# Loading the norm rows ahead of the weights, and taking half of the residual work earlier, in the two output-projection stages of a fused two-model block

## The chip, the cores and the metric

The kernel runs on one core of one Trainium2 chip. The metric is the time of one execution on the device, in microseconds (us); smaller is better. All data and arithmetic are float32; matmul operands are stored as pairs of rounded fp32 parts ("hi" and "lo"), so that one product takes three matmuls.

## The reference, cut to what matters

A sequence of 256 tokens of width 1024 goes through a first block (a conformer convolution and a gated FFN) and then through two layers of a second block. Each layer is FFN, mixer, output projection, FFN. The changed code is the output projection with its residual:

```python
x = layer_norm(ALPHA * x + 0.5 * swiglu(x, ...), ln_g[i, 0], ln_b[i, 0])      # FFN 1
...                                                                          # mixer -> heads
heads = jnp.concatenate([mix, memory_attention(mq, mem_k, mem_v)], axis=-1)
x = layer_norm(ALPHA * x + heads @ w_out[i], ln_g[i, 1], ln_b[i, 1])          # output projection
x = layer_norm(ALPHA * x + 0.5 * swiglu(x, ...), ln_g[i, 2], ln_b[i, 2])      # FFN 2
```

## The kernel before, in words

The program is a row of blocks; at the end of each, all engines meet. The output projection of layer 0 (after the RWKV mixer) and that of layer 1 (after the stick-breaking mixer) are the two calls of `output_stage`, called stage A and stage B here. Both do the same work.

**Weights.** All wide weights pass through a ring of two raw buffers `a_raw[:, 0..1]` (1 MB each, 128 partitions x 2048 words). A chunk g is loaded by SyncE (`Ring.load`, L112), its hi part is made by ScalarE (a copy with rounding), its lo part by VectorE (raw minus hi), and TensorE multiplies with both. `Ring.load(g)` waits until the lo part of chunk g-2 is made, since that frees the raw buffer. The output weights `w_out` are four chunks, g0 to g0+3, called chunks 0 to 3 here. Chunks 0 and 1 were loaded and split in the stage before. In the output stage, SyncE loads chunks 2 and 3 and then chunks 4 and 5, which are the first two weight chunks of the FFN that follows (each as two DMAs of 512 KB, gate and up). The loads of chunks 2 and 3 wait for nothing in this stage; that of chunk 4 waits for the lo part of chunk 2, that of chunk 5 for the lo part of chunk 3.

**Split buffers.** The parts of chunk 2 go to `b_parts`, which is free. Those of chunk 3 take the place of chunk 1's, those of chunk 4 the place of chunk 0's. So ScalarE's hi part of chunk 3 waits until TensorE is done with chunk 1 (`ring_a.used`). ScalarE runs chunks 2, 3 and 4 in this order at L1533, VectorE follows at L1548.

**The residual.** x lies in `x_tok` (tokens on partitions, two tiles t = 0, 1) as the plain normalized value of the norm before. Its gain and bias must still be applied before `ALPHA * x` is added. For this, two rows of 1024 words, `ln_g` and `ln_b`, are loaded with a broadcast to all 128 partitions (`load_row`, L297, 512 KB written by each), and `residual(t)` does a multiply (L1539) and an add (L1540) of 128x1024 on VectorE, for each t. The buffer `rows` holds masks of the mixer in stage A until that mixer is over.

**The end of the stage.** TensorE accumulates four output blocks (t, half n). Blocks 0 to 2 are finished first, then block 3's part from chunk 2, then the transposes of token tile 0 (`turn_tokens`, L371), and only then block 3's part from chunk 3. VectorE goes on, right behind the lo part of chunk 4, with `norm_dve_side`: for each block the sum with `ALPHA * x` (L326) and its statistics (L328), then mean and variance, a square root on ScalarE (L339), a reciprocal, and the scaling of the low half (L351), for which the transposes wait. All engines run their instructions in the order of the program text.

Of the kernel before, what the change touches and what calls it, by code (L numbers as in the profile page):

```python
# [210 lines left out]
def build_program(nc, A, out):  # L211
    with ExitStack() as ctx:
# [3 lines left out]
        def sem(name):  # L216
            return ctx.enter_context(nc.semaphore(name))
# [28 lines left out]
        def carve(*shapes, limit=arena_words):  # L246

            at, got = 0, []
            for shape in shapes:
                n = math.prod(shape)  # L250
                ap = arena[:, at:at + n]
                if len(shape) == 2:
                    ap = ap.rearrange("p (a b) -> p a b", a=shape[0])
                elif len(shape) == 3:
                    ap = ap.rearrange("p (a b c) -> p a b c", a=shape[0], b=shape[1])
                got.append(ap)
                at += n
            assert at <= limit, (at, limit)
            return got
# [20 lines left out]
        rows_loaded = sem("rows_loaded")  # L280
# [14 lines left out]
        def load_row(eng, slot, vec):  # L295

            eng.dma_start(rows[:, slot], vec.partition_broadcast(P)).then_inc(rows_loaded, 16)  # L297
# [68 lines left out]
        def turn_tokens(pe, i, t):  # L366

            for h, ready in enumerate((low_ready[t], high_ready[t])):
                pe.wait_ge(ready, i + 1)
                for k in range(4 * h, 4 * h + 4):  # L370
                    ins = pe.transpose(turned_at(i, t, k), x_tok[:, t, k * P:(k + 1) * P], ident[:])  # L371
                ins.then_inc(token_turned[t], 1)
# [55 lines left out]
        def norm_act_side(act, i, yb, scale, norm):  # L428

            block_root(act, i, 0, scale)  # L430
            block_high(act, i, 0, yb)
            first_affine(act, i, yb, norm, range(6),
                         lambda o, x, g, b: act.activation(o, x, ACT.Identity, bias=b, scale=g))
            block_root(act, i, 1, scale)
            block_high(act, i, 1, yb)

        def norm_dve_side(dve, i, yb, scale, norm, end):

            block_sum(dve, i, 0, 0, yb, scale, end)
            block_sum(dve, i, 0, 1, yb, scale, end)  # L440
            block_stat(dve, 0)
            block_low(dve, i, 0, yb)
            block_sum(dve, i, 1, 0, yb, scale, end)
            block_sum(dve, i, 1, 1, yb, scale, end)
            block_stat(dve, 1)
            first_affine(dve, i, yb, norm, range(6, KD),
                         lambda o, x, g, b: dve.tensor_scalar(o, x, g, b, ALU.mult, ALU.add))
            block_low(dve, i, 1, yb)

        def take_tokens(i, yb, norm):  # L450

            first = slice(0, P)

            def on_act(act):
                tokens_act(act, i, 1, yb, norm)

            def on_dve(dve):
                if norm is None:
                    tokens_dve(dve, i, 0, yb, norm)
                else:  # L460
                    dve.wait_ge(token_scaled, 2 * i)
                    dve.tensor_copy(actT[:, 0, :, first], token_view(yb, 0)).then_inc(token_hi[0], 1)  # L462
                    dve.wait_ge(token_hi[0], i + 1)
                    dve.tensor_tensor(actT[:, 1, 0:4, first], token_view(yb, 0)[:, 0:4],  # L464
                                      actT[:, 0, 0:4, first].bitcast(F32), ALU.subtract).then_inc(token_lo[0], 1)
                tokens_dve(dve, i, 1, yb, norm)

            def on_pool(pool):
                if norm is not None:
                    pool.wait_ge(token_hi[0], i + 1)  # L470
                    pool.tensor_tensor(actT[:, 1, 4:KD, first], token_view(yb, 0)[:, 4:KD],  # L471
                                       actT[:, 0, 4:KD, first].bitcast(F32), ALU.subtract).then_inc(token_lo[0], 1)
            return on_act, on_dve, i, norm, on_pool

        def norm_row(which, i):
            return A[f"ln_{which}_2"][i // 3, i % 3]
# [1030 lines left out]
        def output_stage(i, hand, got_norm):  # L1507

            g0 = sec["w_out", i]
            norm = 3 * i + 1  # L1510
            yb, = carve((NT, D))
            rows_count[0] += 32
            rows_at = rows_count[0]

            def parts_of(c, s):
                return b_parts[:, s].rearrange("p a n -> p (a n)") if c == 2 else a_parts[:, (g0 + c) % 2, s]

            with nc.Block() as block:
                @block.sync
                def _(sp):  # L1520
                    for g in range(g0 + 2, g0 + 4 + 2):
                        ring_a.load(sp, g)
                        if g == g0 + 3:
                            load_row(sp, 0, norm_row("g", got_norm))
                            load_row(sp, 1, norm_row("b", got_norm))

                @block.scalar
                def _(act):
                    for c in range(2, 5):
                        act.wait_ge(ring_a.loaded[(g0 + c) % 2], ring_a.load_no[g0 + c])  # L1530
                        if c > 2:
                            act.wait_ge(ring_a.used, g0 + (2 if c == 3 else 1))
                        act.activation(parts_of(c, 0), a_raw[:, (g0 + c) % 2], ACT.Copy).then_inc(ring_a.hi_done, 1)  # L1533
                    norm_act_side(act, hand, yb, 1.0, norm)

                @block.vector
                def _(dve):
                    def residual(t):
                        dve_steps.step(dve, dve.tensor_tensor(x_tok[:, t], x_tok[:, t], rows[:, 0], ALU.mult))  # L1539
                        dve_steps.mark(dve.tensor_tensor(x_tok[:, t], x_tok[:, t], rows[:, 1], ALU.add))  # L1540

                    for c in range(2, 5):
                        if c == 3:
                            dve.wait_ge(rows_loaded, rows_at)
                            residual(0)
                            residual(1)
                        dve.wait_ge(ring_a.hi_done, g0 + c + 1)
                        dve.tensor_tensor(parts_of(c, 1), a_raw[:, (g0 + c) % 2], parts_of(c, 0).bitcast(F32),  # L1548
                                          ALU.subtract).then_inc(ring_a.lo_done, 1)
                    dve.wait_ge(dve_steps.sem, dve_steps.n)  # L1550
                    norm_dve_side(dve, hand, yb, 1.0, norm, (ring_a.used, g0 + 4))

                @block.tensor
                def _(pe):
                    for c in range(2):
                        ring_a.wait_split(pe, g0 + c)
                        for t in range(NT):
                            for n in range(2):
                                ins = down_chunk(pe, parts_of, c, t, n)
                        ins.then_inc(ring_a.used, 1)  # L1560
                    ring_a.wait_split(pe, g0 + 2)
                    for t, n in BLOCKS[:3]:
                        down_chunk(pe, parts_of, 2, t, n)
                    ring_a.wait_split(pe, g0 + 3)
                    for t, n in BLOCKS[:3]:
                        down_chunk(pe, parts_of, 3, t, n).then_inc(acc_done, 1)
                    down_chunk(pe, parts_of, 2, *BLOCKS[3]).then_inc(ring_a.used, 1)
                    turn_tokens(pe, hand, 0)
                    down_chunk(pe, parts_of, 3, *BLOCKS[3]).then_inc(ring_a.used, 1)
            return take_tokens(hand, yb, norm)  # L1570

        def down_chunk(pe, parts_of, c, t, n):

            for k in range(2 * c, 2 * c + 2):
                w = [parts_of(c, s)[:, (k % 2) * D + n * 512:(k % 2) * D + n * 512 + 512] for s in range(2)]
                ins = mm3(pe, acc[t][:, HALF[n]], [actT[:, s, k, t * P:(t + 1) * P] for s in range(2)], w,
                          k == 0, k == KD - 1)
            return ins
# [951 lines left out]
```

## Time and profile before

| | |
|---|---|
| median of three runs | 1601.83 us (1598.4 to 1602.2) |
| the profiled execution, its time | 1602.2 us |
| its span in the profile | 1600.4 us |
| mean granted TensorE clock | 0.944 of full speed |
| TensorE (matmul) busy | 1443.6 us, 90% of the span |
| VectorE busy | 962.0 us, 60% |
| ScalarE busy | 674.6 us, 42% |
| GpSimd busy | 171.1 us, 11% |
| stage A, from the first SyncE load to TensorE's last block | 833.8 to 860.8 us |
| stage B, the same | 1371.3 to 1397.5 us |

The span runs from the first to the last instruction that the profile shows; the execution's own time has 1.8 us more around it. The idle time of an engine counts only where another engine waits for what it does next, so the stages are read below in order of time rather than by busy shares. In rows of the timeline, "x2" merges two instructions that follow each other, and the bracket gives how long the engine had been idle and what released it.

### The profile page before, as it was taken

The numbers are of one execution on the slowest core, as the hardware profiler recorded it, in microseconds if no ns is written. First come the engines' busy times: TensorE is split into PE (matmuls) and PEld (weight loads), VectorE is DVE, ScalarE is ACT, GpSimd is POOL, SyncE is SP. The second block draws the span as 40 slices with busy tenths as digits, with TensorE's granted clock in tenths as the row PEclk, the third lists the DMA queues.
The fourth block names the chain that finished last, engine by engine and source line by source line (L and its number), as shares of the span: only waits on it lengthen the run. The fifth ranks groups of instructions, "written<-read, shape, count | busy, mean of one in ns | idle before, by whom it ended". The sixth has DMA issues, their size and how long they took to land. (4 is left out here: it accounts for less than half of the span.)

```text
span 1600.4 us, 30883 instructions
## 1 busy us (share of the span) xinstructions
PE 1443.6 (90%) x12484; PEld 1306.9 (82%) x12484; DVE 962.0 (60%) x1275; ACT 674.6 (42%) x848; POOL 171.1 (11%) x190
## 2 busy tenths in 40 slices
PE   6999799997999988938858999989999895799997
PEld 4877599996999977928857999979999794689997
DVE  2666566667555565675537565666556646665656
ACT  4445545454333446442324334443343444343332
POOL 1450133320000022003300000000000002000000
PEclk8999899999999989969978999999999997899999
DMA  9964366663666625300015666656665340376662
GB/s 364 334 206 184 118 208 187 184 196 119 190 181 194 184 93 178 132 1 4 3 52 178 192 183 184 192 170 178 193 186 184 125 153 13 132 211 189 181 193 93
DMA packets 297971, 257.71 MB, mean 161 GB/s; under 512 B 7072, under 2 KB 274336, under 8 KB 294816
## 3 DMA queue, kind: packets, MB, share of 16 engines
q1 hardware_dynamic: 297888, 256.49, 51.4%
q8 instruction: 66, 1.08, 0.3%
q14 instruction: 17, 0.14, 0.0%
HBM read 255.42 MB, written 1.05 MB: 160 GB/s over the span
## 5 line engine op out<-in xcount | busy, mean ns | idle before, releaser
L137 PE MATMUL ps<-actT,a_parts 128*128 128x256 f32 x2176 | 620.4, 285 | 19.4 <-DVE actT L403 11.1
L138 PE MATMUL ps<-actT,a_parts 128*128 128x256 f32 x2176 | 615.3, 283 | 0.0
L139 PE MATMUL ps<-actT,a_parts 128*128 128x256 f32 x2176 | 614.6, 282 | 0.0
L137 PEld LDWEIGHTS ps<-actT,a_parts 128*128 128x128 f32 x2176 | 417.3, 192 | 32.1 <-issue 20.5
L138 PEld LDWEIGHTS ps<-actT,a_parts 128*128 128x128 f32 x2176 | 417.7, 192 | 4.2
L139 PEld LDWEIGHTS ps<-actT,a_parts 128*128 128x128 f32 x2176 | 417.1, 192 | 0.0
L1117 DVE TENSOR_TENSOR a_parts<-a_raw,a_parts 128x2048 fp32r<-128x2048 f32 x100 | 239.6, 2396 | 57.9 <-ACT a_parts L1114 57.7
L1114 ACT ACTIVATE a_parts<-a_raw 128x2048 fp32r<-128x2048 f32 x100 | 190.3, 1903 | 0.0
L1131 DVE TENSOR_TENSOR b_parts<-b_raw,b_parts 128x1024 fp32r<-128x1024 f32 x72 | 88.2, 1225 | 160.5 <-ACT b_parts L1128 160.5
L1128 ACT ACTIVATE b_parts<-b_raw 128x1024 fp32r<-128x1024 f32 x90 | 95.3, 1059 | 171.1 <-PE ps L139 171.1
L139 PE MATMUL ps<-b_parts,hid 128*128 128x512 f32 x400 | 158.3, 396 | 0.0
L138 PE MATMUL ps<-b_parts,hid 128*128 128x512 f32 x400 | 158.3, 396 | 0.0
L137 PE MATMUL ps<-b_parts,hid 128*128 128x512 f32 x400 | 158.0, 395 | 0.0
L122 DVE TENSOR_TENSOR a_parts<-a_raw,a_parts 128x2048 fp32r<-128x2048 f32 x47 | 110.4, 2348 | 65.9 <-ACT a_parts L118 65.9
L1165 ACT ACTIVATE arena<-ps 128x256 f32<-128x256 f32 x88 | 33.8, 384 | 256.8 <-PE ps L139 256.8
L118 ACT ACTIVATE a_parts<-a_raw 128x2048 fp32r<-128x2048 f32 x48 | 91.6, 1911 | 24.1 <-PEq L1790 8.9
L1192 DVE TENSOR_TENSOR arena<-arena,ps 128x256 f32<-128x256 f32 x88 | 37.0, 421 | 91.7 <-ACT arena L1165 91.7
L139 PEld LDWEIGHTS ps<-b_parts,hid 128*128 128x128 f32 x400 | 75.1, 188 | 18.1
L138 PEld LDWEIGHTS ps<-b_parts,hid 128*128 128x128 f32 x400 | 75.1, 188 | 13.8
L137 PEld LDWEIGHTS ps<-b_parts,hid 128*128 128x128 f32 x400 | 75.1, 188 | 13.9
L471 POOL TENSOR_TENSOR actT<-arena,actT 128x512 fp32r<-128x512 f32 x5 | 8.9, 1771 | 721.3 <-DVE actT L462 721.3
L137 PE MATMUL ps<-a_parts,actT 128*128 128x512 f32 (+1 forms) x128 | 48.3, 378 | 12.9 <-PEq L1930 9.7
(344 smaller groups left out, 1743.3 us busy)
## 6 DMA issues: line engine op xcount, KB each, us to landing
a_raw<-in_ffn_w_gate SPq DMA_DIRECT2D x88, 512.0 KB, 4.0
a_raw<-in_ffn_w_up SPq DMA_DIRECT2D x88, 512.0 KB, 5.2
b_raw<-in_ffn_w_down SPq DMA_DIRECT2D x88, 512.0 KB, 3.2
arena<-in_mod_w SPq DMA_DIRECT2D x24, 1024.0 KB, 7.9
a_raw<-in_f_up_w SPq DMA_DIRECT2D x44, 512.0 KB, 5.0
b_raw<-in_f_down_w SPq DMA_DIRECT2D x22, 512.0 KB, 3.2
a_raw<-in_rwkv_w_in SPq DMA_DIRECT2D x10, 1024.0 KB, 5.2
a_raw<-in_sb_w_in SPq DMA_DIRECT2D x10, 1024.0 KB, 5.3
```

The source lines that it names most:

```text
L118: act.activation(self.parts[:, g % 2, 0], self.raw[:, g % 2], ACT.Copy).then_inc(self.hi_done, 1)
L122: dve.tensor_tensor(self.parts[:, g % 2, 1], self.raw[:, g % 2], self.parts[:, g % 2, 0].bitcast(F32), ALU.subtract).then_inc(self.lo_done, 1)
L137: pe.matmul(out, lhs[0], rhs[0], start=start, stop=False)
L138: pe.matmul(out, lhs[0], rhs[1], start=False, stop=False)
L139: return pe.matmul(out, lhs[1], rhs[0], start=False, stop=stop)
L471: pool.tensor_tensor(actT[:, 1, 4:KD, first], token_view(yb, 0)[:, 4:KD], actT[:, 0, 4:KD, first].bitcast(F32), ALU.subtract).then_inc(tok ...
L1114: act.activation(a_parts[:, q, 0], a_raw[:, q], ACT.Copy).then_inc(ring_a.hi_done, 1)
L1117: dve.tensor_tensor(a_parts[:, q, 1], a_raw[:, q], a_parts[:, q, 0].bitcast(F32), ALU.subtract).then_inc(ring_a.lo_done, 1)
L1128: act.activation(b_of(q, j)[:, 0], b_raw[:, q], ACT.Copy).then_inc(ring_b.hi_done, 1)
L1131: lo.tensor_tensor(b_of(q, j)[:, 1], b_raw[:, q], b_of(q, j)[:, 0].bitcast(F32), ALU.subtract).then_inc(ring_b.lo_done, 1)
L1165: act.activation(cg[:, q], gate, ACT.Silu).then_inc(gated, 1)
L1192: dve.tensor_tensor(hf[:, q], cg[:, q], up, ALU.mult).then_inc(f_step, 1)
```

## The change

In `output_stage` alone, two things move. SyncE issues the two row loads ahead of the four weight loads instead of behind the second. VectorE waits for the rows and does `residual(0)` ahead of the lo part of chunk 2; `residual(1)` stays between the lo parts of chunks 2 and 3. Nothing is added or left out.

```diff
                 @block.sync
                 def _(sp):
+                    load_row(sp, 0, norm_row("g", got_norm))
+                    load_row(sp, 1, norm_row("b", got_norm))
                     for g in range(g0 + 2, g0 + 4 + 2):
                         ring_a.load(sp, g)
-                        if g == g0 + 3:
-                            load_row(sp, 0, norm_row("g", got_norm))
-                            load_row(sp, 1, norm_row("b", got_norm))
...
+                    dve.wait_ge(rows_loaded, rows_at)
+                    residual(0)
                     for c in range(2, 5):
                         if c == 3:
-                            dve.wait_ge(rows_loaded, rows_at)
-                            residual(0)
                             residual(1)
                         dve.wait_ge(ring_a.hi_done, g0 + c + 1)
                         dve.tensor_tensor(parts_of(c, 1), a_raw[:, (g0 + c) % 2], parts_of(c, 0).bitcast(F32),
```

## Rows read from the trace of the kernel before

**Rows 1.** The page: span, and busy time by engine.

```profile
span 1600.4 us, 30883 instructions
PE 1443.6 (90%) x12484; PEld 1306.9 (82%) x12484; DVE 962.0 (60%) x1275; ACT 674.6 (42%) x848; POOL 171.1 (11%) x190
```

**Rows 2.** Timeline, SyncE, stage A: start us, us, what, [idle before <- releaser].

```profile
833.78 0.88 SPq L112 DMA_DIRECT2D a_raw<-in_w_out  x2
...
842.89 0.38 SPq L112 DMA_DIRECT2D a_raw<-in_ffn_w_gate  x1
843.31 0.58 SPq L112 DMA_DIRECT2D a_raw<-in_ffn_w_up  x1
```

**Rows 3.** DMA issues of stage A: KB, us from issue to landing.

```profile
a_raw<-in_w_out SPq DMA_DIRECT2D x1, 1024.0 KB, 4.8
...
a_raw<-in_w_out SPq DMA_DIRECT2D x1, 1024.0 KB, 7.0
...
a_raw<-in_ffn_w_up SPq DMA_DIRECT2D x1, 512.0 KB, 5.0
```

**Rows 4.** Timeline, ScalarE, stage A.

```profile
838.62 1.92 ACT L1533 ACTIVATE b_parts<-a_raw 128x2048 fp32r<-128x2048 f32 x1 [7.11 <-DMA a_raw<-in_w_out]
847.68 3.72 ACT L1533 ACTIVATE a_parts<-a_raw 128x2048 fp32r<-128x2048 f32 x2 [7.14 <-PE ps L139]
```

**Rows 5.** Timeline, VectorE, stage A.

```profile
840.57 2.29 DVE L1548 TENSOR_TENSOR b_parts<-a_raw,b_parts 128x2048 fp32r<-128x2048 f32 x1 [7.27 <-ACT b_parts L1533]
843.72 1.23 DVE L1539 TENSOR_TENSOR x_tok<-x_tok,rows 128x1024 f32<-128x1024 f32 x1 [0.86 <-DMA rows<-in_ln_b]
...
849.63 4.49 DVE L1548 TENSOR_TENSOR a_parts<-a_raw,a_parts 128x2048 fp32r<-128x2048 f32 x2 [1.03 <-ACT a_parts L1533]
854.04 0.68 DVE L326 SCALAR_TENSOR_TENSOR arena<-x_tok,ps 128x512 f32<-128x512 f32 x1
...
860.78 0.69 DVE L326 SCALAR_TENSOR_TENSOR arena<-x_tok,ps 128x512 f32<-128x512 f32 x1 [1.27 <-PE ps L139]
```

**Rows 6.** Timeline, TensorE, stage A: first matmul on chunk 2, first transposes.

```profile
847.42 0.40 PE L137 MATMUL ps<-b_parts,actT 128*128 128x512 f32 x1
...
858.25 1.10 PE L371 MATMUL ps<-ident,x_tok 128*128 128x128 f32 x8 [0.41 <-DVE x_tok L351]
```

**Rows 7.** Timeline, SyncE, ScalarE and VectorE, stage B.

```profile
1371.28 0.88 SPq L112 DMA_DIRECT2D a_raw<-in_w_out  x2
...
1380.74 0.58 SPq L112 DMA_DIRECT2D a_raw<-in_ffn_w_up  x1
...
1384.45 3.73 ACT L1533 ACTIVATE a_parts<-a_raw 128x2048 fp32r<-128x2048 f32 x2 [6.48 <-PE ps L139]
...
1386.41 4.49 DVE L1548 TENSOR_TENSOR a_parts<-a_raw,a_parts 128x2048 fp32r<-128x2048 f32 x2 [0.36 <-ACT a_parts L1533]
```

**Rows 8.** DMA issues of stage B: the second output chunk, and up.

```profile
a_raw<-in_w_out SPq DMA_DIRECT2D x1, 1024.0 KB, 6.9
...
a_raw<-in_ffn_w_up SPq DMA_DIRECT2D x1, 512.0 KB, 5.2
```

**Rows 9.** The FFN block behind stage A: its row loads, issue and landing.

```profile
864.41 0.34 SPq L297 DMA_DIRECT2D rows<-in_ln_g  x1
864.80 0.43 SPq L297 DMA_DIRECT2D rows<-in_ln_b  x1
...
rows<-in_ln_b SPq DMA_DIRECT2D x1, 512.0 KB, 5.6
```

**Rows 10.** Windows behind both stages: us, busy (x) by engine, PEclk, DMA share, GB/s.

```profile
862.00:863.00 1.00, 0.00 (x0) 0.00 (x0) 0.97 (x5) 0.29 (x1) 0.00 (x0) 0.92 0.00 0
...
873.00:874.00 1.00, 1.00 (x11) 1.00 (x10) 1.00 (x2) 0.00 (x0) 0.00 (x0) 0.96 0.06 16
...
1402.00:1403.00 1.00, 0.30 (x3) 0.05 (x1) 1.00 (x3) 1.00 (x4) 1.00 (x1) 0.57 0.83 274
...
1408.00:1409.00 1.00, 1.00 (x7) 1.00 (x6) 1.00 (x2) 1.00 (x1) 0.00 (x0) 0.51 1.19 312
```

## The prediction

> **What bounds the kernel now.** I read the page first. TensorE is busy for 1443.6 of 1600.4 us [rows 1], so time is won or lost only where TensorE waits. The change touches two stretches of about 27 us, so shares of the whole say little, and I went on to the timeline of each engine in stage A and then in stage B.
>
> In stage A the reader should follow chunk 3 first. ScalarE starts its hi part at 847.68, released by TensorE, after 7.14 us of idle time [rows 4]. TensorE has just gone from chunk 1 to chunk 2, whose first matmul starts at 847.42 [rows 6]. VectorE starts the lo part at 849.63, and the 1.03 us before it are a wait for that hi part [rows 5]. So at this point VectorE has time over and the residual is not what is waited for. Stage B is the same with a smaller margin: the hi part starts at 1384.45 behind TensorE, and VectorE idles 0.36 us for it before 1386.41 [rows 7].
>
> Then comes the end of the stage. The lo parts of chunks 3 and 4 run back to back until about 854.1, and the first block sum starts at 854.04, with no idle time between [rows 5]. The transposes of tile 0 start at 858.25 after TensorE idled 0.41 us for VectorE's L351 [rows 6], and the last block sum at 860.78 waits for TensorE in turn [rows 5]. So from the lo part of chunk 4 onward there is one chain, VectorE to TensorE to VectorE, with nothing to spare: what delays chunk 4's lo part delays the end of the stage by as much.
>
> **Step 1, the residual work.** Four VectorE instructions of about 1.23 us remain four. Two of them move ahead of chunk 2's lo part. Before, chunk 3's lo part was released by ScalarE, and that by TensorE, so taking 2.45 us out of this gap brings it forward by nothing. It gains 0, and the work that hides it is TensorE's on chunks 0 and 1.
>
> **Step 2, the DMA order.** SyncE issues two row loads of 512 KB ahead of chunk 2, so its weight loads are issued about 0.9 us later. That issue delay costs nothing, because the row bytes keep the DMA engines busy. The bytes themselves cost something. The first 1 MB of the stage lands 4.8 us after its issue and the second 1 MB 7.0 us after its own [rows 3]. The pair is issued within 0.88 us [rows 2], so the second lands about 0.44 + 7.0 = 7.44 us after the first issue. After the change the rows take the first place and chunk 2 the second. In stage A the rows are there at 833.78 + 4.8 = 838.6, and chunk 2 at 833.78 + 7.44 = 841.2 instead of 838.6. In stage B it is 0.44 + 6.9 = 7.34 [rows 8], from 1371.28 [rows 7], so 1378.6.
>
> Chunk 3 takes the third place, which the rows had. They let VectorE start at 843.72 [rows 5], so chunk 3 is there by then, 4 us ahead of the hi part that waits for TensorE at 847.68 [rows 4]. It costs nothing.
>
> **Step 3, chunk 2.** From the start of the hi part to that of the lo part it is 840.57 - 838.62 = 1.95 us [rows 4, 5], and the lo part takes 2.29 us [rows 5]. Stage A: 841.2 + 1.95 = 843.2, then 845.5. `residual(0)`, which now stands ahead, runs from 838.6 to 841.1, before the hi part is done, so it delays nothing. TensorE wants chunk 2 at 847.42 [rows 6], 1.9 us later. Stage B: 1378.6, 1380.55, 1382.85; TensorE wants it at about 1384.2 (0.26 us ahead of ScalarE's 1384.45, as in stage A), 1.3 us later. So chunk 2 still arrives in time. `residual(1)` ends 2.45 us behind it, at 848.0 and 1385.3, still before the lo parts of chunk 3 (849.63 and 1386.41).
>
> **Step 4, chunk 4: here it costs.** Its load waits for chunk 2's lo part. Its second half, up, is issued 0.45 us behind the end of that lo part (840.57 + 2.29 = 842.86, against 843.31) [rows 2, 5] and lands 5.0 us after that in stage A [rows 3] and 5.2 in stage B [rows 8].
> - Stage A before: landed 843.31 + 5.0 = 848.3, and the hi part started at about 849.5 behind that of chunk 3, so it was covered by 1.2 us. After: issued 845.95, landed 850.95, hi part until 852.9, lo part from 852.95. Before, the lo part started 2.2 us behind 849.63 [rows 5], at 851.85. The delay is 1.1 us.
> - Stage B before: landed 1380.74 + 5.2 = 1385.9 [rows 7, 8] against a start at about 1386.3, covered by only 0.4 us. After: issued 1383.3, landed 1388.5, lo part from 1390.5, instead of 1386.41 + 2.2 = 1388.6. The delay is 1.9 us.
>
> Behind this lo part VectorE has the block sums queued, and the chain above passes the delay on in full. Chunk 5's load waits for chunk 3's lo part, which does not move.
>
> **The sum.** 0 + 0 + 0 + 1.1 + 1.9 = +3.0 us. Against the profiled execution (1602.2 us, a span of 1600.4 and 1.8 around it) that is 1605.2 us. The median of the runs shown is 0.4 lower, so I forecast 1604.9 us, or +0.19%.
>
> The term that no row shows directly is chunk 2's landing behind the rows. From below it is 0 later, if its bytes get through as if the rows were not there; then nothing is delayed. From above, the row loads of the FFN block behind stage A landed at 864.80 + 5.6 = 870.4, which is 6.0 us after their first issue at 864.41 [rows 9], instead of 4.8; that makes each stage 1.2 us worse. I take the place in the queue, 7.4 us, since the same number of bytes in the same stretch took that in both stages.
>
> The Trainium skill (DMA: Bandwidth & Descriptors, section "Anatomy of one DMA — SWDGE (gpsimd) path") fits a DMA's time as 2.0 us plus bytes over 436 GB/s, for another issue path than this one. For the 2 MB up to chunk 2's end this is 6.8 us, against 7.44 and 7.34 from the rows; by it each delay would shrink by 0.6 and the sum, an estimate, would be +1.8 us instead of +3.0.
>
> **The rivals.**
> - *The delay stays covered.* Chunk 2 is held up by less than the 1.2 and 0.4 us that cover chunk 4 now. For it speaks that DMAs in one queue overlap. Against it, 2 MB took 7.4 us twice. It gives 0, so 1601.8 us.
> - *Slower in a way that can be measured: broadcast rows that land late.* The mechanism is step 2 with the price of rows 9. All terms of step 4 grow by 1.2 us, to 2.3 and 3.1, so +5.4 us and 1607.2. Chunk 2's lo part would then end at 846.7 and 1384.05, still just ahead of TensorE. For it speaks that these are the same two loads; against it, those of the FFN block share the engines with gate and up loads right behind them, while here w_out follows. It passes 0.3% once the rows hold chunk 2 up by more than 0.9 us beyond step 2 in each stage (3.0 + 2 x 0.9 = 4.8).
> - *Faster.* If the freed VectorE time brought chunk 3's lo part forward, the most to win is VectorE's wait there, 1.03 and 0.36 us: -1.4 us, 1600.4. Against it stands that these waits are for ScalarE, and its for TensorE.
> - *The clock.* Behind stage A the granted clock is at half level from about 862.8 to 873.1, and behind stage B from 1402.1 to 1409.0 [rows 10]: 10.3 against 6.9 us for the same code. A later arrival may shift such a stretch. Half of the 3.4 us of difference, 1.7 us, is the most I give it, of either sign. If the clock fell already in the longer wait ahead of the transposes, the six matmuls of the last block, 0.40 us each at the full level [rows 6], would take at most 2.4 us more in that stage. It gives up to 1607.3.
>
> **How the numbers follow.** Chunk 4 late as in step 4: 0.60, 1604.9 us, its own range 1603 to 1606.5. Covered: 0.18. Late rows: 0.12. Faster: 0.04. A clock that changes by more than 1 us: 0.06. The range of 1600.2 to 1607.4 goes from the faster case to the late rows and leaves out under 2 in 10. A measurement of this kernel can tell a change of about 0.3%, 4.8 us, from none. Slower by over that takes most of the late rows and of the clock's bad side, 0.13; faster by over that has no mechanism here, 0.03; the rest, 0.84, is within 0.3%.
>
> **What would show it.** In the profile after: rows landed 4.8 us after the stage's first issue; chunk 2's hi part at 841.2 instead of 838.6; `residual(0)` done before it ends; chunk 3's lo part where it was, 15.9 us from the stage's first issue in A (849.63 - 833.78); ScalarE idle between the hi parts of chunks 3 and 4, released by the DMA of up, for 1.4 and 2.2 us; the two lo parts no longer back to back; and TensorE's wait ahead of the transposes grown from 0.41 to about 1.5 and 2.3 us. The prediction is wrong if chunk 2 does not land later, if chunk 4's hi part still follows chunk 3's at once, or if TensorE waits for chunk 2.

## The result, and the profile after

The changed kernel takes 1608.94 us (median of six runs, 1607.71 to 1615.22); the kernel before, run beside it, 1600.89 us. The ratio is 1.0055, with a 95% interval of 1.0041 to 1.0070: slower, by 6.6 to 11 us. The forecast was 1604.9 us, with 1600.2 to 1607.4 as its range, and "within 0.3%" as by far the likeliest. The time lies outside that range.

All shapes and counts on the page are those of before; only the span grew, by 5.8 us in the profiled execution (its own time is 1607.9 us):

```profile
span 1606.2 us, 30883 instructions
PE 1441.4 (90%) x12484; PEld 1306.4 (81%) x12484; DVE 963.6 (60%) x1275; ACT 675.2 (42%) x848; POOL 168.8 (11%) x190
```

Next are the timelines of SyncE, ScalarE, VectorE and TensorE in stage A, which answer to [rows 2], [rows 4], [rows 5] and [rows 6]. Lines 1532, 1538 and 1547 of the changed kernel are 1533, 1539 and 1548 of before.

```profile
832.61 0.34 SPq L297 DMA_DIRECT2D rows<-in_ln_g  x1
833.00 0.43 SPq L297 DMA_DIRECT2D rows<-in_ln_b  x1
833.47 0.94 SPq L112 DMA_DIRECT2D a_raw<-in_w_out  x2
...
845.77 0.58 SPq L112 DMA_DIRECT2D a_raw<-in_ffn_w_up  x1
...
841.08 1.92 ACT L1532 ACTIVATE b_parts<-a_raw 128x2048 fp32r<-128x2048 f32 x1 [10.75 <-DMA a_raw<-in_w_out]
846.75 1.92 ACT L1532 ACTIVATE a_parts<-a_raw 128x2048 fp32r<-128x2048 f32 x1 [3.75 <-PE ps L139]
851.13 1.92 ACT L1532 ACTIVATE a_parts<-a_raw 128x2048 fp32r<-128x2048 f32 x1 [2.46 <-DMA a_raw<-in_ffn_w_up]
...
838.54 1.23 DVE L1538 TENSOR_TENSOR x_tok<-x_tok,rows 128x1024 f32<-128x1024 f32 x1 [6.41 <-DMA rows<-in_ln_b]
...
843.04 2.29 DVE L1547 TENSOR_TENSOR b_parts<-a_raw,b_parts 128x2048 fp32r<-128x2048 f32 x1 [2.02 <-ACT b_parts L1532]
...
848.70 2.29 DVE L1547 TENSOR_TENSOR a_parts<-a_raw,a_parts 128x2048 fp32r<-128x2048 f32 x1 [0.98 <-ACT a_parts L1532]
853.08 2.29 DVE L1547 TENSOR_TENSOR a_parts<-a_raw,a_parts 128x2048 fp32r<-128x2048 f32 x1 [2.09 <-ACT a_parts L1532]
855.29 0.68 DVE L326 SCALAR_TENSOR_TENSOR arena<-x_tok,ps 128x512 f32<-128x512 f32 x1
...
859.49 1.09 PE L371 MATMUL ps<-ident,x_tok 128*128 128x128 f32 x8 [2.57 <-DVE x_tok L351]
```

Read it against step 4 of the prediction. ScalarE's third hi part, that of chunk 4, followed the second at once before. Now ScalarE idles 2.46 us for the DMA of up. The two lo parts on VectorE are no longer back to back (2.09 us between them), and TensorE's wait ahead of the transposes went from 0.41 to 2.57 us. The signs that the prediction named are there, larger than it had them: ScalarE's idle time was to be 1.4 and 2.2 us and is 2.46 and 3.01 us (stages A and B), TensorE's wait was to be 1.5 and 2.3 us and is 2.57 and 3.11 us. Stages start at different times in different executions (stage A at 828.2 to 834.2 us in the thirteen profiles told of here), so all that follows is counted from the first DMA issue of the stage. A block sum is VectorE's instruction at L326; the first is that of block (0, 0), the last that of block (1, 1):

| | hi of chunk 2 | first block sum | last block sum |
|---|---|---|---|
| before, stage A / B | 4.84 / 4.78 | 20.26 / 19.54 | 27.00 / 26.27 |
| changed, A / B | 8.47 / 8.63 | 22.68 / 22.72 | 29.41 / 29.45 |

The first block sum is 2.42 and 3.18 us late, 5.6 us in all, and the last one the same 5.6. The span grew by about as much, 5.8 us, but that the two agree so well is partly luck: what lies outside the two stages (a stage taken from its first DMA issue to its last block sum) takes 1543.2 to 1547.3 us in the thirteen profiles, whatever the kernel. The stage times are the better evidence, and the ratio of many runs the measure of the whole. Step 2 had chunk 2 at 7.44 and 7.34; it came about 1.0 and 1.3 us later than that.

### The profile page after: what moved, and what is told of

Read it like the earlier page. It is cut to its first block and busy times, and to the rows that moved or that the text cites. A ratio compares the mean times of both kernels' runs of the same rounds, so it can differ in the third digit from the quotient of the medians.

```text
span 1606.2 us, 30883 instructions
## 1 busy us (share of the span) xinstructions
PE 1441.4 (90%) x12484; PEld 1306.4 (81%) x12484; DVE 963.6 (60%) x1275; ACT 675.2 (42%) x848; POOL 168.8 (11%) x190
```

## The experiments

The comparisons below count stage times in the same way. Each kernel has one profile, the changed kernel two, so a stage time is one observation; "late" is against the one profile of the kernel before that is shown above. A ratio is taken against the kernel before, run on the same chip, with its 95% interval in brackets.

**The changed kernel again.**

> The changed kernel once more, beside the others on one chip. Its profile showed the hi part of chunk 4 waiting for its load and everything behind it 2.42 us later in stage A and 3.18 us in stage B, counted from each stage's first DMA issue. Theory (the chain through chunk 4's lo part): +5.6 us of delay, so a median about 5.6 to 8 us above the kernel before. Rival (something else, outside the two stages, adds 2 to 3 us more, since the medians differ by 8.05 us): the ratio stays near 1.0055.

Ratio 1.0049 (1.0032 to 1.0065). First block sums at 23.23 and 22.65, chunk 2's hi part at 9.24 and 8.56. So chunk 2's place in time varies from one execution to the next, and stage A loses 3.0 us here. The first block sums are late by 6.1 us in all, and in stage B something was added behind them. The next lines are VectorE's last block sum, TensorE's transposes and last block in stage B, and two windows of them (the last three columns are the granted TensorE clock, DMA share and GB/s):

```profile
1402.33 0.69 DVE L326 SCALAR_TENSOR_TENSOR arena<-x_tok,ps 128x512 f32<-128x512 f32 x1 [2.19 <-PE ps L139]
...
1398.86 1.09 PE L371 MATMUL ps<-ident,x_tok 128*128 128x128 f32 x8 [3.21 <-DVE x_tok L351]
1399.71 0.48 PE L137 MATMUL ps<-a_parts,actT 128*128 128x512 f32 x1
...
1401.23 0.63 PE L138 MATMUL ps<-a_parts,actT 128*128 128x512 f32 x1
...
1398.86:1399.70 0.84, 0.84 (x8) 0.84 (x9) 0.81 (x2) 0.34 (x1) 0.00 (x0) 1.00 0.00 0
...
1400.50:1402.30 1.80, 1.79 (x5) 0.88 (x3) 0.00 (x0) 1.70 (x5) 0.00 (x0) 0.50 0.00 0
```

TensorE had waited 3.21 us ahead of the transposes. They ran at the full level (1.00 in the first window), and in the last block the granted clock fell to the half level (0.50). Its matmuls take 0.63 us there instead of 0.40 us [rows 6]; the 0.48 us of the first is what the first one of this block takes at the full level too. VectorE's wait for them is 2.19 us instead of 1.27 [rows 5], 0.9 us more. The last block sums of this profile are late by 7.0 us, which lies within the intervals of both measurements of this kernel (6.6 to 11 and 5.1 to 10.4 us). The 5.6 us of the first profile do not reach 6.6: how much the clock, or anything else, adds in a typical run was not counted.

**Only the DMA order.** The kernel before with the diff's SyncE part alone.

```diff
+                    load_row(sp, 0, norm_row("g", got_norm))
+                    load_row(sp, 1, norm_row("b", got_norm))
                     for g in range(g0 + 2, g0 + 4 + 2):
                         ring_a.load(sp, g)
-                        if g == g0 + 3:
-                            load_row(sp, 0, norm_row("g", got_norm))
-                            load_row(sp, 1, norm_row("b", got_norm))
```

> Only the DMA order is changed (rows first); VectorE's order is that of before. Theory: all of the loss comes from chunk 2 landing about 8.5 us after the stage's first issue, so the same +5.6 us as the changed kernel. VectorE does both residuals behind the lo part of chunk 2, so chunk 3's lo part should start about 1.5 us (A) and 2.2 us (B) later than in the changed kernel and TensorE waits there instead of ahead of the transposes, with the end of the stage where the changed kernel has it. Rival (VectorE's new order is what costs, by waiting for the rows): then this is like before, within 1 us. Rival (taking residual 0 earlier saves time): then this is slower than the changed kernel by 1 us or more.

Ratio 1.0040 (1.0026 to 1.0055). First block sums at 22.46 and 22.72: the changed kernel's loss, to 0.2 us. Chunk 3's lo part starts at 17.39 and 17.64 (changed: 16.09 and 15.59), and TensorE's waits, summed over stage A (who waits for whom: us, times, longest), show the loss in two pieces:

```profile
PE ps L137 <- DVE a_parts L1547: 1.5, 1, 1.5
PE ps L371 <- DVE x_tok L351: 1.1, 1, 1.1
```

So the DMA order alone makes the loss, with VectorE's order of before. (This profile's span is only 1601.8 us, since stage A began at 828.2; the loss is read from the stages and the ratio.) VectorE's new order takes away a wait for chunk 3 that the DMA order would make, but what ends last is chunk 4's load, so nothing is won by it.

**Only VectorE's order.** The rows are loaded third, as before.

```diff
+                    dve.wait_ge(rows_loaded, rows_at)
+                    residual(0)
                     for c in range(2, 5):
                         if c == 3:
-                            dve.wait_ge(rows_loaded, rows_at)
-                            residual(0)
                             residual(1)
```

> Only VectorE's order is changed: it waits for the rows and does residual 0 ahead of chunk 2's lo part, while the rows are loaded third as before. Theory: the rows land 9.9 us after the first issue, residual 0 ends at 12.4, chunk 2's lo part at 14.7, one to two microseconds after TensorE wants it, and chunk 4 is issued at about 14.7; the first block sum is late by 4.1 us (A) and 4.9 us (B), +9 us in all, ratio about 1.0055: slower than the changed kernel. Rival (VectorE's order does not matter, the DMA order alone does): like before.

Ratio 1.0099 (1.0080 to 1.0117), the slowest of all. The first block sums are at 25.50 and 24.51, late by 5.2 and 5.0 us. Waiting for the rows makes chunk 2's lo part so late that TensorE waits for it, 1.8 and 1.7 us, where before it did not wait for chunk 2 at all. In stage A the rows also came at 11.0 instead of 9.9. The clock adds the rest: in both stages the transposes and half or all of the last block ran at the half level (0.50) after waits of 3.5 us, and the last block sums came 4.15 and 4.71 us behind the third one instead of 2.7. Together the last block sums are 13.7 us late (the span is 1614.1). I had priced 9 us, without the clock.

**Rows between chunks 2 and 3.** The kernel before, with its row loads one place earlier.

```diff
-                        if g == g0 + 3:
+                        if g == g0 + 2:
```

> The rows are loaded between chunk 2 and chunk 3; VectorE's order is that of before. Theory: chunk 2 lands 4.8 us after the stage's first issue as before, chunk 4 is issued as before, and chunk 3, now third, still lands ahead of TensorE's release of its hi part: no change against before, within 0.15%. VectorE's residual starts right behind chunk 2's lo part or up to 0.9 us earlier than before, which gains nothing. Rival (row loads early in the stage disturb the kernel wherever they stand): slower by 2 us or more.

Ratio 1.0007 (0.9997 to 1.0016). Chunk 2's hi part at 4.84 and 4.98, the residual 0.9 us earlier than before in stage A, and VectorE's wait ahead of chunk 3's lo part 1.96 us instead of 1.03. The time won on the residual comes out as a longer wait there. In stage A the first block sum stands at 20.24, as before. In stage B it stands at 20.10, 0.56 us late, with ScalarE's hi part of chunk 3 released by TensorE 0.57 us later than before (13.74 against 13.17): so much a stage time can move by TensorE's pace on chunks 0 and 1 alone. The ratio shows no harm from early rows if chunk 2 stays ahead of them, and no good either.

**Chunk 4's lo part taken off the chain, twice.** First by GpSimd, then on VectorE behind the sum of block (1, 0). Both are the changed kernel otherwise.

```diff
-                    for c in range(2, 5):
+                    for c in range(2, 4):
...
+                @block.gpsimd
+                def _(pool):
+                    pool.wait_ge(ring_a.lo_done, g0 + 4)
+                    pool.wait_ge(ring_a.hi_done, g0 + 5)
+                    for h in range(2):
+                        w = slice(h * BCH, (h + 1) * BCH)
+                        ins = pool.tensor_tensor(parts_of(4, 1)[:, w], a_raw[:, (g0 + 4) % 2, w],
+                                                 parts_of(4, 0)[:, w].bitcast(F32), ALU.subtract)
+                    ins.then_inc(ring_a.lo_done, 1)
```

> The changed kernel, but the lo part of chunk 4 is made by GpSimd (two instructions of 128x1024, about 2.5 us each by the kernel's own rows) instead of VectorE, so that the block sums no longer stand behind it. Theory: chunk 4's load is as late as in the changed kernel, but nobody on the chain waits for it: the first block sum starts within 0.5 us of TensorE's block 0, the whole 5.6 us come back and up to 0.5 us per stage more; ratio to before 0.999 to 1.001. Rival (the loss is elsewhere, for example in the clock or in TensorE's order): still 1.003 or more. Rival (GpSimd's work slows VectorE down): part of it stays, seen in longer L326 and L328.

```diff
             block_sum(dve, i, 1, 0, yb, scale, end)
+            between()
             block_sum(dve, i, 1, 1, yb, scale, end)
...
+                    norm_dve_side(dve, hand, yb, 1.0, norm, (ring_a.used, g0 + 4), lambda: lo(4))
```

Here `lo(4)` makes the lo part of chunk 4.

> The changed kernel, but the lo part of chunk 4 stays on VectorE and moves behind the sum of block (1, 0), where VectorE waited 1.3 us for TensorE. Theory (the delay goes through chunk 4's lo part alone): the first block sum starts 20.0 us (A) and about 19.3 us (B) after the stage's first issue although chunk 4's load is as late as ever, and the last block sum is late by only 0.8 to 1.0 us in each stage since the lo part no longer fits its gap: +1.7 us against before, 3.9 us less than the changed kernel; ratio about 1.001. Rival (VectorE was slowed by GpSimd in the other experiment because chunk 4's delay matters elsewhere too): no better than 1.003.

With GpSimd the ratio is 1.0023 (1.0009 to 1.0036). The first block sums start at 20.04 and 19.21, released by TensorE after 1.8 us of waiting, with chunk 4's hi part as late as ever (18.54 and 18.53). So the delay is off the chain. But the last block sums are 1.4 and 2.7 us late. The greater part came back in one VectorE instruction of each stage. The lines are VectorE's and GpSimd's in stage B:

```profile
1394.61 0.25 DVE L349 SCALAR_TENSOR_TENSOR stats<-stats 128x1 f32<-128x1 f32 x1
1394.78 2.65 DVE L351 TENSOR_SCALAR x_tok<-arena,stats 128x512 f32<-128x512 f32 x1
...
1392.44 4.69 POOL L1541 TENSOR_TENSOR a_parts<-a_raw,a_parts 128x1024 fp32r<-128x1024 f32 x2 [36.26 <-ACT a_parts L1532]
```

In stage B the clock took the rest: it fell to the half level in the last block after TensorE had waited 2.33 us ahead of the transposes, and the last sum came 3.46 us behind the third instead of 2.67.

On VectorE between the sums the ratio is 0.9998 (0.9985 to 1.0011): the loss is gone as far as can be measured, although chunk 2 landed later in stage A than in any other profile (hi part at 9.84) and chunk 4's load with it. So late, chunk 2's lo part made TensorE wait 0.34 us. VectorE's lines of stage A:

```profile
852.28 0.69 DVE L326 SCALAR_TENSOR_TENSOR arena<-x_tok,ps 128x512 f32<-128x512 f32 x1 [1.84 <-PE ps L139]
...
857.68 2.27 DVE L1546 TENSOR_TENSOR a_parts<-a_raw,a_parts 128x2048 fp32r<-128x2048 f32 x1
859.88 0.68 DVE L326 SCALAR_TENSOR_TENSOR arena<-x_tok,ps 128x512 f32<-128x512 f32 x1
```

The last block sum is 1.1 and 0.6 us late (28.11 and 26.84), as the lo part overfills its gap. The expectation had 0.8 to 1.0 and a ratio of 1.001. This pair shows the chain: the same late load costs 5.6 us when VectorE waits for it ahead of the block sums, and 1.7 us, too little to measure, when it waits behind.

**What makes chunk 2 so late behind the two row loads.** Three kernels put something else ahead of chunk 2. In the first, chunk 3 goes ahead and the rows stay third:

```diff
-                    for g in range(g0 + 2, g0 + 4 + 2):
+                    for g in (g0 + 3, g0 + 2, g0 + 4, g0 + 5):
                         ring_a.load(sp, g)
-                        if g == g0 + 3:
+                        if g == g0 + 2:
```

> The kernel before, but chunk 3 is loaded ahead of chunk 2; the rows stay third and VectorE's order is that of before. So chunk 2 has 1 MB of plain weights ahead of it instead of 1 MB of rows. Theory (second place in the queue costs 2.5 us by bytes alone, the rest of the changed kernel's delay is the rows'): chunk 2's hi part about 7.4 us after the stage's first issue, delays of 1.1 and 1.9 us, +3.0 us in all. Rival (any chunk 2 behind 1 MB lands at 8.5): +5.6 us.

In the second, two loads of 512 KB without a broadcast; in the third, one load of 1 MB into the same place (`then_inc(rows_loaded, 32)`):

```diff
-                    load_row(sp, 0, norm_row("g", got_norm))
-                    load_row(sp, 1, norm_row("b", got_norm))
+                    for slot in range(2):
+                        sp.dma_start(rows[:, slot], A["w_out_2"][i][slot * P:(slot + 1) * P, :]).then_inc(rows_loaded, 16)
```

> The changed kernel, but the two row loads read 128 different rows of w_out (512 KB each, one row of 4 KB for each partition) instead of one row for all partitions; so the values in the rows are other numbers, and the output is not the reference's. Place, size and destination are the same. In the changed kernel the DMA rate fell to 220 to 270 GB/s for 2.5 us while the rows moved at the head of the queue. Theory A (reading one row for all partitions is what is slow at the head): now 420 GB/s all through, rows landed about 4.8 us after the first issue and chunk 2's hi part at 7.4 instead of 8.5, and the loss is the 1.1 + 1.9 = 3.0 us of the prediction; ratio about 1.002. Theory B (two loads of 512 KB at the head are slow whatever they read): chunk 2 at 8.5 as in the changed kernel, and +5.6 us.

```diff
-                    load_row(sp, 0, norm_row("g", got_norm))
-                    load_row(sp, 1, norm_row("b", got_norm))
+                    sp.dma_start(rows, A["w_out_2"][i][0:2 * P, :].rearrange("(k p) n -> p k n", p=P))\
+                        .then_inc(rows_loaded, 32)
```

> The changed kernel with one load of 1 MB (256 rows of w_out, as chunk 0 has them) into the same two row buffers, ahead of chunk 2; the rows hold other numbers, so the output is not the reference's. The two plain loads of 512 KB put chunk 2 at 8.7 to 8.9 us, chunk 3 of 1 MB ahead put it at 7.5 to 7.7. Theory A (two short loads at the head instead of one long): chunk 2's hi part at 7.5 to 7.7 us. Theory B (the destination, or the wait that VectorE makes for it, is what differs): 8.6 or more.

| ahead of chunk 2 | hi of chunk 2, A / B | first block sum, A / B | ratio |
|---|---|---|---|
| two row loads (changed kernel) | 8.47 / 8.63 | 22.68 / 22.72 | 1.0055 (1.0041 to 1.0070) |
| two plain loads of 512 KB | 8.93 / 8.67 | 23.09 / 22.95 | 1.0039 (1.0025 to 1.0054) |
| one plain load of 1 MB | 7.52 / 7.50 | 21.77 / 21.80 | one run only |
| chunk 3, 1 MB | 7.65 / 7.45 | 21.78 / 21.48 | 1.0029 (1.0020 to 1.0039) |

The intervals of the ratios overlap; what tells these kernels apart is where chunk 2 stands in their profiles. The same bytes in one load put chunk 2 at 7.5 us, where step 2 had it, and in two loads at 8.4 us or more, broadcast or not. In the ten stages with the two row loads first it ranged from 8.44 to 9.84. Four stages in all, three of them with two loads first, have one more DMA packet between the loads, which the view of the DMA queues lists as "instruction" (16 KB): the stages at 9.24 and 9.84, that at 8.93 in the table, and stage A of "only VectorE's order", where chunk 2 stood at 5.92 instead of 4.84. They are the latest of their kinds. That this packet is the cause is a guess. Without it the row loads first give 8.44 to 8.69.

The two kinds of two loads do not come to the same lateness by the same way. The DMA rate of the changed kernel (windows of 0.5 us: the last column is GB/s) dips to 221 while the row loads move:

```profile
835.60:836.10 0.50, 0.50 (x2) 0.40 (x2) 0.00 (x0) 0.00 (x0) 0.00 (x0) 0.50 1.05 254
836.10:836.60 0.50, 0.50 (x2) 0.34 (x2) 0.00 (x0) 0.00 (x0) 0.00 (x0) 0.50 1.01 221
...
838.10:838.60 0.50, 0.50 (x4) 0.37 (x3) 0.06 (x1) 0.00 (x0) 0.00 (x0) 0.81 1.01 418
```

The two row loads among the DMA issues of the same kernel (the last column is us from issue to landing):

```profile
rows<-in_ln_g SPq DMA_DIRECT2D x1, 512.0 KB, 3.7
...
rows<-in_ln_b SPq DMA_DIRECT2D x1, 512.0 KB, 5.5
```

In [rows 3] the first load of 1 MB lands after 4.8 us; these two, of the same size together, need 5.9 from the first issue. In the same stretch there is no dip with one plain load of 1 MB ahead (first two lines), nor with two plain loads (last two lines, stage A):

```profile
835.33:835.83 0.50, 0.50 (x3) 0.40 (x2) 0.00 (x0) 0.00 (x0) 0.00 (x0) 0.50 0.96 393
836.33:836.83 0.50, 0.50 (x2) 0.40 (x2) 0.00 (x0) 0.00 (x0) 0.00 (x0) 0.50 1.05 434
...
836.01:836.51 0.50, 0.50 (x2) 0.40 (x2) 0.00 (x0) 0.00 (x0) 0.00 (x0) 0.50 0.98 385
836.51:837.01 0.50, 0.50 (x2) 0.33 (x1) 0.00 (x0) 0.00 (x0) 0.00 (x0) 0.50 0.98 401
```

The packets begun in the first 4.8 us of a stage say the same: 0.97 to 1.04 MB in all ten stages with the two row loads first, 1.22 to 1.34 MB in the fourteen others that load from SyncE alone, the two with plain loads among them (1.30 and 1.25). So the low rate at the head of the queue goes with the broadcast. (With two plain loads stage B has one window of 197 GB/s, 4.0 to 4.5 us after the first issue.) But taking the broadcast away did not bring chunk 2 forward. With two plain loads more bytes had to move before chunk 2 had landed. The lines give the packets from the first issue to that landing, for two plain loads (stages A and B) and for one (A):

```profile
DMA packets 779, 3.01 MB, mean 337 GB/s; under 512 B 48, under 2 KB 48, under 8 KB 778
DMA packets 709, 2.71 MB, mean 313 GB/s; under 512 B 48, under 2 KB 48, under 8 KB 709
...
DMA packets 616, 2.39 MB, mean 319 GB/s; under 512 B 32, under 2 KB 32, under 8 KB 616
```

Of these, 2.1 MB (2 x 1024 KB) are the loads ahead and chunk 2; the rest can only be chunk 3's, which was begun before chunk 2 had landed. In stage B the two plain loads had even landed at 4.6 us, before the 4.8 of one load in [rows 3], and chunk 2 came at 8.67 all the same. Theory A fell: without the broadcast chunk 2 is as late. Theory B had chunk 2's place right, but its reason, that two short loads are slow whatever they read, is not what the rates show. Why chunk 2 ends so late behind two plain loads stays open. One difference was not taken apart: behind two loads chunk 2 is issued at 0.87 us, behind one at 0.41 to 0.50. Why two row loads in third place cost nothing (chunks 2 and 3 and the rows had all landed 9.9 us after the first issue before) is open too.

With chunk 3 ahead, the delays are 1.5 and 1.9 us, where step 4 had 1.1 and 1.9 from nearly the same landing; up's landing, 5.3 us after its issue instead of 5.0, is 0.3 us of the difference in stage A. That is the prediction's arithmetic with the right input.

**Rows on ScalarE's queue.** SyncE's first DMA is chunk 2 again.

```diff
                 @block.scalar
                 def _(act):
+                    load_row(act, 0, norm_row("g", got_norm))
+                    load_row(act, 1, norm_row("b", got_norm))
```

The two `load_row` lines of SyncE's block are gone.

> The changed kernel with the two row loads issued by ScalarE at the start of its block instead of by SyncE, so that SyncE's first DMA is chunk 2. VectorE's order is that of the changed kernel. Theory (the bytes share the DMA engines): rows and chunk 2 move side by side; chunk 2's hi part comes at 6 to 8.5 us, between the 4.8 of before and the changed kernel's, and the delay of the first block sum is 0 to 2 us (A) and 0.5 to 3 us (B). Rival (a second queue gets its own share without holding chunk 2 up): hi part at 5 us and no loss.

Ratio 1.0058 (1.0043 to 1.0074). Chunk 2's hi part starts 7.6 and 7.8 us after its issue, and the rows come only after 8.3 and 8.6 us, so VectorE, which waits for them first, makes chunk 2's lo part later than in the changed kernel (10.7 and 11.0 against 10.4 and 10.6). The two queues' loads moved side by side and both came late: chunk 2 at 7.6 instead of the 4.8 of before, the rows at 8.3 instead of the 5.9 of the changed kernel, with 352 to 430 GB/s for both together between 839 and 841 us, no more than SyncE's queue moved alone. The first block sums stand at 22.82 and 23.00, 6.0 us late in all, and in stage B the clock fell in the last block too (after a wait of 3.45 us), so that the last ones are 7.2 us late.

**A version from what was learnt.** Rows between chunks 2 and 3, residuals as before, and chunk 4's lo part in two halves: one ahead of the block sums, one behind the sum of block (1, 0). The cut shows the halves and the two places.

```diff
+                    def lo4(h):
+                        w = slice(h * BCH, (h + 1) * BCH)
+                        return dve.tensor_tensor(parts_of(4, 1)[:, w], a_raw[:, (g0 + 4) % 2, w],
+                                                 parts_of(4, 0)[:, w].bitcast(F32), ALU.subtract)
+
+                    dve_steps.mark(lo4(0))
...
+                                  lambda: lo4(1).then_inc(ring_a.lo_done, 1))
```

> A version meant to be at least as good as both: rows loaded between chunk 2 and chunk 3 (chunk 4's load stays early), residuals where the kernel before has them, and the lo part of chunk 4 in two halves of 128x1024: one (about 1.2 us) ahead of the block sums, where VectorE would otherwise wait 1.8 us for TensorE's block 0, the other behind the sum of block (1, 0), in the gap of 1.3 us. Theory: first block sum at 20.0 us (A) and 19.2 to 19.8 us (B) after the stage's first issue, last one at 26.8 and 26.0, so 0.2 to 0.3 us earlier than before in each stage; ratio 0.9985 to 1.001, not to be told from the kernel before, and 0.4% better than the changed kernel. Rival (splitting costs more than it fits): above 1.002.

Ratio 1.0004 (0.9992 to 1.0016): like before, and by the ratios 0.4 to 0.5% better than the changed kernel. The sums stand where they were expected, at 20.03 and 19.25, the last ones at 26.78 and 26.00, 0.2 and 0.3 us earlier than before. VectorE's lines show the first sum waiting for TensorE and the second half filling the gap:

```profile
849.71 1.22 DVE L1555 TENSOR_TENSOR a_parts<-a_raw,a_parts 128x1024 fp32r<-128x1024 f32 x1
851.62 0.69 DVE L326 SCALAR_TENSOR_TENSOR arena<-x_tok,ps 128x512 f32<-128x512 f32 x1 [0.70 <-PE ps L139]
...
857.02 1.21 DVE L1555 TENSOR_TENSOR a_parts<-a_raw,a_parts 128x1024 fp32r<-128x1024 f32 x1
858.37 0.69 DVE L326 SCALAR_TENSOR_TENSOR arena<-x_tok,ps 128x512 f32<-128x512 f32 x1
```

Up to its last block TensorE now waits for VectorE only 0.2 us, for the parts of chunk 3, so in this stretch there is little left to win in VectorE's order. TensorE's 3.7 us of waiting behind the last block, which stand in the kernel before too, were not looked into.

## Why the prediction was wrong, point by point

- **The bound and the chain: right.** What delays chunk 4's lo part delays the end of the stage by as much: first and last block sums are late by the same 5.6 us. Moving that lo part behind the sums took the loss away.
- **Step 1, residual work gains 0: right.** With the rows between the chunks, the residual was 0.9 us earlier in stage A and VectorE waited 0.9 us longer.
- **Step 2, the DMA order: here it failed.** "I take the place in the queue, 7.4 us, since the same number of bytes in the same stretch took that in both stages." The same number of bytes took 7.5 us only in one load. In two loads chunk 2 came at 8.47 and 8.63 us. The term had the right mechanism and was 1.0 us too small in stage A and 1.3 us in stage B. The upper bound (6.0 us for the rows, 1.2 more in each stage) was the right row to take: rows 9 are the same two loads at the head of a queue. I set it aside because of the gate and up loads behind them. In the changed kernel the rows landed at 5.9 and 5.8. That the bound came out so near is partly luck: it had chunk 2 late because the rows are, and behind two plain loads that had landed at 4.6 us chunk 2 was as late. Step 2 also had chunk 3 there by 843.72, 9.9 us after the first issue; it landed at 11.0 and 11.1, still 3.2 and 2.5 us ahead of its hi part, so this cost nothing.
- **Step 3, chunk 2 in time for TensorE: right.** TensorE's wait for the parts of chunk 3 stayed at 0.2 us and there was none for chunk 2. The margin is small: with chunk 2 at 9.84 us, in another kernel with the same loads, TensorE waited 0.34 us for it.
- **Step 4, chunk 4: right, with the wrong input.** 1.1 and 1.9 became 2.4 and 3.2: the missing 1.0 and 1.3, and 0.3 us more for up's landing in stage A (5.3 instead of 5.0). The sum was 5.6 us instead of 3.0, which alone puts the forecast at 1601.8 + 5.6 = 1607.4 us, the top of the range. The median is 1.5 us above that. What makes up these 1.5 us in a typical run is not shown; the clock, below, is one candidate, and the spread outside the stages is another.
- **The rivals.** The late rows, priced at +5.4 us and given 0.12, are what happened. The delay did not stay covered, and there was no gain. The clock did not fall ahead of the last block's end in the first profile. In the second it did, in stage B, and cost 0.9 us there; with VectorE's order alone it cost 1.5 and 2.0 us. The prediction had bounded this at 2.4 us but treated it as an alternative to the late rows. It goes with them: the late load makes the wait ahead of the transposes longer, and the clock fell behind such waits in seven stages of the experiments. Both together pass the top of the range.
- **The Trainium skill's fit** (DMA: Bandwidth & Descriptors, "Anatomy of one DMA — SWDGE (gpsimd) path"), 6.8 us for 2 MB, missed further: 7.5 us was measured with one load ahead and 8.5 with two. The page gives the fit for one DMA; taken over the 2 MB of several loads it has no term for how they are cut, and here that was worth 1 us.

## What to carry to other kernels

A load that is moved up in a queue can delay everything it passes; follow the passed load to the next one that waits for its buffer, since the bill came two loads later (chunk 2's delay was covered, chunk 4's was not). Take the landing time from a row with the same loads in the same place, not from one with the same bytes. And work for the next stage that stands ahead of this stage's last chain, like chunk 4's lo part, can turn a late load into a late stage; in the gap of the chain it cost nothing here that could be measured.

## What was not expected of the hardware

- A load of 1 MB stood about 1 us later behind two loads of 512 KB than behind one of 1 MB (hi part at 8.4 to 9.8 against 7.5 to 7.7 us), with or without a broadcast.
- Two broadcast row loads at the head of the queue lowered the DMA rate to 221 to 254 GB/s, with the engines' busy share at 1.0; two plain loads of the same size, in stage A, ran at 385 to 401 GB/s in the same stretch.
- A VectorE instruction of 0.54 us (L351) took 2.65 us, until GpSimd's subtraction ended, and in stage A L349 took 1.77 instead of 0.16; the block sums beside the same subtraction kept their 0.69 us. The Trainium skill (SBUF — State Buffer, "SBUF: two separate sides") says that GpSimd and some kinds of VectorE instruction take a shared port for a whole instruction, and the other waits. The trace agrees, with these numbers.
- The length of TensorE's wait ahead of the transposes did not alone decide its clock. The granted clock stayed at the full level after waits of 2.57 and 3.11 us (the changed kernel), 3.12 us (its second profile, stage A), 2.97 us (two plain loads, A) and 3.00 us (rows on ScalarE's queue, A). It fell to the half level at the start of the last block or in it after 2.33 us (chunk 4's lo part on GpSimd, B), 2.86 us (one plain load first, B), 3.21 us (the changed kernel's second profile, B), 3.45 us (rows on ScalarE's queue, B) and 3.51 us (two plain loads, B), and already in the transposes after 3.46 and 3.54 us (VectorE's order alone).
